# Routing the last tile in halves, the first rows group by group, and an earlier ask for the second expert's weights

## The reference

```python
x = x + mix @ w_out[l]                                    # 512 x 1024
xn = rmsnorm(x, ffn_norm_w)
logits = xn @ w_router + b_router                         # 512 x 32
top_val, top_idx = lax.top_k(logits, 4); gates = softmax(top_val)
# every (token, expert) pair, sorted by expert:
hid = x_blk @ w_gate_up[e] + b_gate_up[e]                 # 1024 -> 2048
gate, up = min(hid[:, :1024], 7), clip(hid[:, 1024:], -7, 7)
y = ((up + 1) * gate * sigmoid(1.702 * gate)) @ w_down[e] + b_down[e]
x = x + segment_sum(y * gate_of_pair, token)
out = rmsnorm(x, final_norm_w)
```

## Time and profile before

| | |
|---|---|
| time, median of 3 runs | 1390.28 us (1388.48 to 1390.84) |
| profiled execution | 1390.32 us, span 1388.6 us |
| TensorE (PE) busy | 1232.1 us (89%) |
| VectorE (DVE) busy | 683.6 us (49%) |
| ScalarE (ACT) busy | 220.4 us (16%) |
| GpSimd (POOL) busy | 327.2 us (24%) |
| chain that ended last | PE 53%, DMA 36%, DVE 7% |
| HBM read, written | 445.02 MB, 14.81 MB |
| mean granted TensorE clock | 0.978 |

### The profile page before, as it was taken

How to read it: one execution, slowest core, us unless ns; L and a number is a source line. 1 busy time by engine, 2 the same in 40 slices (tenths; PEclk the granted TensorE clock), 3 DMA queues, 4 the chain that set the end, 5 groups by cost and what they waited for, 6 DMA issues and landing times.

```text
span 1388.6 us, 32055 instructions
## 1 busy us (share of the span) xinstructions
PE 1232.1 (89%) x12818; PEld 540.9 (39%) x12819; DVE 683.6 (49%) x1365; ACT 220.4 (16%) x435; POOL 327.2 (24%) x435
## 2 busy tenths in 40 slices
PE   6999999999599999799899899788987887879992
PEld 3444555564234443244433334233432332334331
DVE  2898884444543453436433334445443334354428
ACT  3125545313100010000010000000100000001103
POOL 6002111001222233222323222222222222222221
PEclk9999999999799999999999999999999999999996
DMA  9212000511689999999999999999999999999996
GB/s 307 87 61 92 1 31 1 201 73 46 252 339 401 410 418 424 425 427 426 425 426 424 424 427 427 424 427 425 425 424 426 425 426 427 426 425 425 379 409 248
DMA packets 58142, 455.33 MB, mean 328 GB/s; under 512 B 12060, under 2 KB 22356, under 8 KB 32982
## 3 DMA queue, kind: packets, MB, share of 16 engines
q1 hardware_dynamic: 44660, 434.13, 75.5%
q0 software_dynamic: 11664, 18.95, 3.8%
q10 hardware_dynamic: 1778, 1.69, 0.4%
HBM read 445.02 MB, written 14.81 MB: 331 GB/s over the span
## 4 chain that ended last, share of the span: by engine, by line
PE 53%; DMA 36%; DVE 7%; issue 2%; ACT 2%; POOL 1%; SPq 0%; POOLq 0%; DVEq 0%; ACTq 0%
DMA ring<-in_w_gate_up_dram 26%; PE bank L2166 23%; PE bank L2219 11%; DMA dslots<-in_w_down_dram 8%; PE bank L1826 6%; PE bank L2017 4%; DVE dslots L1145 2%; PE bank L1821 2%; DVE hbuf L1720 1%; PE bank L1894 1%; PE bank L1901 1%; DMA rows<-in_x_dram 1%; DMA wq<-xn_rows,idx_in 1%; PE bank L2152 1%; PE bank L1982 1%
## 5 line engine op out<-in xcount | busy, mean ns | idle before, releaser
L2166 PE MATMUL bank<-ring,wq 128*32 128x512 f32 x4992 | 561.2, 598 | 69.6 <-DMA ring<-in_w_gate_up_dram 66.9
L2166 PEld LDWEIGHTS bank<-ring,wq 128*32 128x32 f32 x4992 | 167.8, 110 | 422.7 <-issue 419.7
L2219 PE MATMUL bank<-dslots,intra 128*32 128x256 f32 x5056 | 281.7, 380 | 24.8 <-DMA dslots<-in_w_down_dram 24.6
L2219 PEld LDWEIGHTS bank<-dslots,intra 128*32 128x32 f32 x5056 | 165.0, 110 | 151.4 <-issue 53.9
L1533 DVE TENSOR_REDUCE small<-bank 128x4 f32<-128x8 f32 x33 | 5.5, 166 | 415.7 <-PE bank L2130 415.7
L1012 ACT ACTIVATE zrows<-intra 128x1024 f32<-128x1024 f32 x31 | 32.8, 1058 | 796.8 <-DVE intra L1626 796.8
L1826 PE MATMUL bank<-hbuf,ring 128*128 128x512 f32 x320 | 148.5, 604 | 0.1
L619 POOL COPY idx_in<-idx 128x4 int32 (+1 forms) x32 | 11.9, 371 | 557.8 <-DVE wq L1511 535.4
L1598 DVE STREAM_TRANSPOSE wq<-bank 128x512 f32<-128x512 f32 x124 | 77.8, 685 | 71.0 <-PE bank L2166 71.0
L624 POOL DMA_INDIRECT wq<-xn_rows,idx_in x82 | 101.7, 1241 | 44.2 <-POOL idx_in L619 27.8
L629 POOL DMA_INDIRECT y_rows<-rows,idx_out x79 | 81.2, 1027 | 55.8 <-issue 43.6
(11 more groups left out here) (302 smaller groups left out, 900.6 us busy)
## 6 DMA issues: line engine op xcount, KB each, us to landing
ring<-in_w_gate_up_dram SPq DMA_DIRECT2D x127, 2048.0 KB, 24.9
dslots<-in_w_down_dram SPq DMA_DIRECT2D x61, 2048.0 KB, 25.4
ring<-in_w_in_dram SPq DMA_DIRECT2D x12, 1024.0 KB, 12.4
ring<-in_w_out_dram SPq DMA_DIRECT2D x4, 1024.0 KB, 4.9
ring<-in_w_down_dram SPq DMA_DIRECT2D x4, 1024.0 KB, 24.8
dslots<-y_rows SPq DMA_DIRECT2D x2, 2048.0 KB, 20.2
rows<-in_x_dram SPq DMA_DIRECT2D x4, 512.0 KB, 9.8
hbuf<-in_x_dram SPq DMA_DIRECT2D x4, 512.0 KB, 5.5
```

What stands on the lines that cost most here:

```text
L2166: ins = M(bank[g][GROUP * j:GROUP * (j + 1), :], x[:, g, c * GROUP:(c + 1) * GROUP], w[:, :, j * QD:(j + 1) * QD], start=(c == 0), stop=(c ...
L2219: ins = M(b[GROUP * j:GROUP * (j + 1), col:col + QD], actT[:, g, c * GROUP:(c + 1) * GROUP], w[:, cc, j * QD:(j + 1) * QD], start=(c == 0 ...
```

## The change

- **Logits.** `logits_turn` is a matmul with the folded identity `fold_e` that adds the four partial sums at once; `route` has no reduce any more. The mask is made by one compare of 4 x 32 and one max-reduce.
- **Last tile in halves.** TensorE transposes the first half of the last tile as soon as the first half of the residual is there. Both halves of the transposes are copied by VectorE, and ScalarE's copy of them goes; ScalarE squares the tile when both halves of the residual are there.
- **Places tile by tile.** Ranks, places, `pos` and the one-hots of expert 0 are made for each tile behind its mask; the rank now counts within the tile. The index matmuls of visit 0 leave out the gates (3 columns instead of 6) and are summed in one bank as the tiles come; the gates follow in matmuls of their own (`first_gates`) behind c0 = 0 of visit 0. `split` of the last tile moves behind the gathers.
- **First rows group by group.** The first gather has a semaphore of its own (`lead_in`); groups 0 and 1 are transposed one by one, 2 and 3 together, and TensorE starts with group 0.
- **Index matmuls of visit 1** stand behind c0 = 2 of visit 0 instead of c0 = 0; VectorE makes expert 1's one-hots behind the first transposes.
- **Weights.** SP asks for 1/4 directly behind 0/6, without waiting for the writes of `xn`.
- **Last rows.** The last tile's write to `xn_dram` is issued on ScalarE's queue. Several small loads are counted on other semaphores.

```diff
             gate_up(0, 6)
-            for i in range(2):
-                sp.wait_ge(xn_out[i], 16 * T // 2)
             gate_up(1, 4)
-            sp.wait_ge(first_in, 32)
+            sp.wait_ge(lead_in, 16)
+            sp.wait_ge(first_in, 16)
             sp.wait_ge(gathered, 32)
...
             pool.wait_ge(idx_ready, 1)
             pool.sem_inc(rows_known, 1)
-            for i in range(2):
-                pool.wait_ge(xn_out[i], 16 * T // 2)
-            for g in range(2):
-                gather(g, idx, first_in)
+            pool.wait_ge(xn_out[0], 32)
+            pool.wait_ge(xn_out[1], 16)
+            pool.wait_ge(wr_in, 80)
+            gather(0, idx, lead_in)
+            gather(1, idx, first_in)
             for g in range(2, GROUPS):
                 gather(g, idx)
+            split(T - 1)
...
             x2_square(3)
-            xnT_copy(3)
             x2_rstd(3)
             lgT_copy(3)
+            act.wait_ge(xn_ready, T)
+            act.dma_start(xn_dram[(T - 1) * P:T * P, :], xn[:, (T - 1) % 2, :]).then_inc(wr_in, 16)
             top_exp(3)
...
-                own.mark(V.tensor_scalar(hits, iota_e, pr4[:, 0:1], None, ALU.is_equal))
-                for k in range(1, TOP_K):
-                    own.settle()
-                    ins = V.scalar_tensor_tensor(out=hits if k < TOP_K - 1 else Msk[:, t, :], in0=iota_e,
-                                                 scalar=pr4[:, k:k + 1], in1=hits, op0=ALU.is_equal, op1=ALU.add)
...
+                own.mark(V.tensor_tensor(same, iota_e.rearrange("p (o e) -> p o e", o=1).to_broadcast([P, TOP_K, E]),
+                                         pr4.rearrange("p (k o) -> p k o", o=1).to_broadcast([P, TOP_K, E]),
+                                         ALU.is_equal))
+                own.settle()
+                V.tensor_reduce(Msk[:, t, :], same.rearrange("p k e -> p e k"), AX_X, ALU.max).then_inc(gate_ready, 1)
+
+            def ranks(t):
+                now = rank[:, t * E:(t + 1) * E]
+                dve.wait_ge(gate_ready, t + 1)
+                own.mark(V.tensor_tensor_scan(now, ones16[:, 0:E], Msk[:, t, :], 0.0, ALU.mult, ALU.add))
+                own.settle()
+                own.mark(V.tensor_scalar(view(tg, 0, T, E, 6)[:, t, :, 2:3].rearrange("p e o -> p (e o)"), now,
+                                         float(PAST), float(-PAST), ALU.mult, ALU.add))
...
             residual(3)
-            dve.wait_ge(xn_turned, T)
-            V.tensor_copy(xnT[(T - 1) % 2][:, 4:8, :], view(bank[4], 0, 4, P)).then_inc(xnT_half, 1)
+            dve.wait_ge(lgT_done, T - 2)
+            for half in range(2):
+                dve.wait_ge(xn_turned, T + half)
+                V.tensor_copy(xnT[(T - 1) % 2][:, 4 * half:4 * half + 4, :], view(bank[3 + half], 0, 4, P)
+                              ).then_inc(xnT_half, 1)
+            ranks(2)
+            places(2, 1, 2)
+            hot_tile(0, 2)
             normed(3)
             route(3)
+            ranks(3)
+            places(3, 1, 3)
+            hot_tile(0, 3)
             gates_of(3)
...
-            dve.wait_ge(first_in, 32)
-            first_turn(0)
+            dve.wait_ge(lead_in, 16)
+            first_turn(0, 1, row_turned)
+            dve.wait_ge(first_in, 16)
+            first_turn(1, 1, xt_ready)
             dve.wait_ge(gathered, 32)
-            first_turn(1)
+            first_turn(2, 2, xt_ready)
+            dve.wait_ge(pos_done, 5)
+            hot(1)
...
                     if first and c0 == 0:
-                        pe.wait_ge(idx_ready, 1)
+                        first_gates()
+                    if first and c0 == 2:
                         idx_mm(1, 2 * T + 1)
```

More of the change, by code:

```diff
@@ L195, in block_kernel @@
         rowf = take(GROUPS)
-        fold = take(2 * H)
+        fold_e = take(E)
+        fold = fold_e[:, 0:2 * H]
         leftf, cnt = take(E), take(E)
@@ L1471, in _ @@
             gates_of(0)
+            ranks(0)
             normed(2)
@@ L1533, in numbers @@
                 mk(V.tensor_reduce(rowf, ps[:, :, 0:2], AX_X, ALU.add))
-                mk(V.tensor_reduce(gates[:, bass.ds(stage * GROUPS, GROUPS)], ps[:, :, 2:5], AX_X, ALU.add))
+                mk(V.tensor_reduce(gates[:, bass.ds(stage * GROUPS, GROUPS)], ps[:, :, 3:6], AX_X, ALU.add))
                 dve.wait_ge(s, c)
@@ L1568, in _ @@
             dve.sem_inc(route_ready, 1)
-            hot(1)
-            dve.wait_ge(hot_ready, 2 * T + 1)
-            lower(1)
             def add_bias(t):
@@ L2054, in logits_turn, with places @@
                     pe.wait_ge(mx_ready, t)
-                TR(bank[6][:, 0:P], lgT, ident).then_inc(lg_done, 1)
+                M(bank[6][:, 0:E], lgT, fold_e, start=True, stop=True).then_inc(lg_done, 1)
+            def places(t):
+                pe.wait_ge(gate_ready, t + 1)
+                for u in range(t + 1):
+                    ins = M(bank[1][:, t * E:(t + 1) * E], tri16 if u == t else ones16, Msk[:, u, :], start=(u == 0),
+                            stop=(u == t))
+                return ins
             su(0)
```

179 lines of the change are left out of this document (100 added, 79 removed).

## The result

The changed kernel takes **1394.93 us** (median of 6 runs, 1394.10 to 1395.38) against 1390.32 us for the kernel before in the same comparison: ratio 1.0035, 95% interval 1.0024 to 1.0045. It is slower by 4.6 us, more than the 0.2% that counts; the forecast was 1391.9 us with a range to 1394.8, and "slower" had a chance of 0.21. The profiled execution took 1394.6 us for a span of 1392.8.

The account below looks back on a forecast made before the run. The prediction took the DMA weight stream to bound the kernel, its end set by the queue's last dry spell. Write and gathers 0.6 plus clock 1.0 gave +1.6 us, forecast 1391.9 us, range 1387.2 to 1394.8.

Parts of the forecast that it names:

- The frame: Whole kernel: the end is the weights' queue's last dry spell, ended by ask 2/0, plus a fixed amount of bytes.
- The routing: Last tile's routing: last normalized tile stays at 357.8 us, row numbers ready at about 361.7, 2.9 us earlier.
- The write: Last rows' write to DRAM: shares the engines with the 1/4 transfer, lands at 365.5; first gather 0.6 us later.
- Visit 0: Start of visit 0's matmuls: at 369.1 us, 2.0 us earlier, from group-by-group rows and a 2.2 us gather.
- The gathers of visit 1: Rows for visit 1: land at 394.6, 1.5 us behind the dry queue; visit 1 starts 0.6 us later, at 397.7.
- rival 2: Visit 1's gathers land a fixed 8.95 us after the ask, at 398.0; time 1394.2 to 1396 us; chance 0.12.
- the quick write (1): Last rows' write takes 3.8 us, first gather 2.9 us earlier; time 1387.4, or 1388.4 if the clock falls; chance 0.17.
- the start of visit 0 decides (3): Visit 1's gathers land before TensorE finishes visit 0, so visit 1 follows at 394.5; time 1387.7 us; chance 0.10.
- Rival 4: Clock falls in full and the write lands at its upper bound; 1393 to 1394 us; a fifth of the main case.
- The clock: TensorE's clock after its 3.9 us stop before visit 1: 2.1 us lost if it falls, else nothing; 1.0 taken.
- The step that failed: Visit 1's start to the end: 2/0 asked for 5.6 us after it, any shift passing one for one to the end.
- The place of the index products: Visit 1's index matmuls two weight rows later in visit 0: last gather starts at 389.0 instead of 385.07.

Follow-up runs that it names:

- e1: Changed kernel plus seven dummy product calls on TensorE in its stop before visit 1; 1397.09 us, ratio 1.0047 to the kernel before.
- a1: Changed kernel, but the ask for weight rows 4 and 5 of visit 1 waits for the last rows' write; 1391.27 us, ratio 1.0008 to before.
- c1: Changed kernel with visit 1's index products and the gate products made before visit 0; 1389.64 us, ratio 0.9996 to the kernel before.
- j1: Kernel before with only visit 1's index products moved behind the second pair of weight rows of visit 0; 1391.96 us, ratio 1.0018.
- d1: Changed kernel with the edits of both a1 and c1; 1388.17 us, ratio 0.9981 to the kernel before.
- g1: d1 plus four dummy products on TensorE while it waits for visit 0's first rows; 1386.66 us, ratio 0.9977 to the kernel before.
- h1: Changed kernel with the sync queue's loop turned, its first ask (2/0) written out ahead of it; 1394.16 us, ratio 1.0036 to before.
- p2: Kernel before with 48 already satisfied waits on TensorE's queue ahead of visit 0; 1390.73 us, ratio 1.0003.
- k2: Changed kernel with e2's three dummy products and h1's turned sync loop; 1393.65 us, ratio 1.0025 to the kernel before.
- e2: Changed kernel plus three dummy product calls on TensorE in its stop before visit 1; 1394.07 us, ratio 1.0028 to the kernel before.
- b1: Kernel before with only the early ask for weight rows 4 and 5 of visit 1, write still on GpSimd's queue; 1391.93 us, ratio 1.0016.
- f1: d1's edits, but weight rows 4 and 5 of visit 1 asked for after the first gathered group lands; 1392.33 us, ratio 1.0015 to before.

## Why the prediction was wrong, step by step

**The frame was right.** The end is the last dry spell of the weights' queue plus a fixed amount of bytes, and that spell ends with 2/0. The rates of the stretches show it, and the fourteen kernels follow it within 1.5 us but for e1. The rate of 410 to 427 GB/s does not hold to the end as the prediction said: the last three slices of the page of before read 379, 409 and 248 GB/s.

**The routing** came out as forecast or a little better: the last normalized tile ends at 357.25 (forecast 357.8, lower bound 357.3), the row numbers are ready at 361.0 (361.7), 6 us before the gather that needs them.

**The write** was forecast to land at 365.5 on the sum of the bytes; it landed at 366.1. (2.9 less 1.2 us is 1.7 us of start and receipt and not 1.5, so the sum's own terms give 365.7.) The Trainium skill (DMA: Bandwidth & Descriptors, Queues, rings and completion order) has each engine take turns between its queues by packets, and the prediction drew from it that the write might be out about a microsecond before the stream. The trace agrees with the turns and not with what was drawn from them. Two DMA views of the changed kernel, 360.5 to 365 us and 365 to 366.1 us (queue: packets, MB, share of the 16 engines; q1 is the stream, q10 the write and the down bias behind it):

```profile
q1 hardware_dynamic: 82, 1.33, 76.6%
q10 hardware_dynamic: 85, 0.35, 18.8%
...
q10 hardware_dynamic: 107, 0.31, 69.4%
q1 hardware_dynamic: 15, 0.00, 0.8%
```

One packet of 4 KB of the write's queue goes for each of 16 KB of the stream. But the first packet of the write shows at 360.7, 3.4 us after the ask (1.7 us in a1, 1.1 before), when 2.87 of the stream's 4.19 MB are through. So the stream is through at 365.0, and the other half of the write's queue goes alone, until 366. The sum of the bytes was the right rule, and the turns gain the write nothing. Why the first packet comes so late isn't shown. In the single microseconds no byte moves any more after 366, and the write lands at 366.09:

```profile
365.00:366.00 1.00, 0.00 (x0) 0.00 (x0) 0.00 (x0) 1.00 (x1) 0.00 (x0) 0.50 0.77 307
366.00:367.00 1.00, 0.00 (x0) 0.00 (x0) 0.00 (x0) 0.10 (x1) 0.00 (x0) 0.50 0.00 0
```

**Visit 0** started at 370.66 instead of 369.1. Its terms were each too small: the write by 0.6, the step to the first gather by 0.15, the transpose by 0.1, and a gather alone in its queue, 2.9 us and not 2.2. The 2.2 came from the last of a train of four; the row that bore on it was the 2.86 of the earlier trace rows.

**The gathers of visit 1** were held to land 1.5 us behind the end of the queue's bytes, whatever the time of the ask. That rule is wrong. In c1, where the last is asked for at 379.49, they land at 388.8 with the stream at 459 GB/s and dry only after 392. What the runs show is a time after the ask that depends on the stream: about 9 us where it runs all or nearly all the while (8.95 before, 9.3 in c1), 5.3 us where it runs dry under way (the changed kernel, and j1 with nothing else changed). So 5.2 us of later ask became 1.6 us of later landing (395.58 for 394.02), 1.0 more than the 394.6 of the forecast, and visit 1 moved by 1.49 us and not 0.6. My rival 2 had the fixed 8.95 us after the ask (398), which holds only for the early asks. The ask itself came at 390.28 and not 389.0, because visit 0 started 1.56 us behind its forecast.

Of the other rivals, the quick write (1) did not come: 8.8 us and not 3.8. That the start of visit 0 decides (3) did not either, but it is what c1, d1 and g1 make true: there visit 1 starts right behind visit 0. Rival 4, the clock falling in full with the write near its upper bound, comes nearest to what was measured, but its 1393 to 1394 has no term for the late ask either.

**The clock** was put at 1.0 us between 0 and 2.1. It fell, and cost 1.69 us. What it does isn't the same from run to run: h1 stood 2.42 us and kept the full clock, a1 stood 2.47 us and lost it. The Trainium skill (TensorE: Matmul & The Clock Gate, Part 1: The HAM clock gate (the "warmup" mystery)) says that the point at which the clock moves varies with the phase of a window that runs free of the kernel; these two stops, of nearly one length with opposite outcomes, are in line with it. It may also be why the runs of a1 and j1 spread over some 5 us; with one trace of each, that isn't shown.

**The step that failed** is the last one of the sum, "it comes 5.6 us after TensorE begins visit 1" and "any shift of it goes one for one to the end". The 5.6 us were taken as a constant. They became 8.98: 1.69 for the clock and 1.67 that the forecast has no term for, the ask coming 2.07 us behind its freed slot instead of 0.40. The forecast's +1.6 against the +4.85 of the ask is then 0.9 too little for the start of visit 1, 0.7 too little for the clock, and 1.7 for the late ask. What makes the ask late stays open. It is 0.40 in the kernel before and between 0.65 and 2.34 in every other kernel; all of these kernels, p2 too, have other code than before, and h1 and k2 do not agree on a cure. e2 shows the other side: taking 1.69 us of low clock away moved the ask by 2.15 us, but the stream's lag at 1300 us by 1.1 and the time by only 0.9.

**The place of the index products** was in the sum only as the loss of an earlier start, a move of visit 1 by 0.6 us. j1 puts its price at 0.18% if it is made alone. What it costs beside the early ask isn't measured by itself: c1 is 5.3 us below the changed kernel, but moves the products further forward than they stood before. The early ask costs 1.9 us alone (b1) and 3.7 us in the company of the other (a1). The two shares overlap, since both feed the same stop of TensorE.

## What to carry to other kernels

When a stream is fed through a ring, find the ask after which its queue stays full, and account for every microsecond from the start of the work that frees its slot to that ask: start, clock, and the delay of the asking queue itself. A short write or gather on which a chain depends can land as late as the bulk transfer beside it or later. Holding the bulk back behind the write helped here (a1 against the changed kernel), behind a gather as well it did not (f1). Place the small products that feed the next gathers ahead of the long work, not in it. Bytes moved by a fixed moment, read from a table of windows, tell where a change was won or lost, and here gave the end of the same execution to about 1.5 us.

## What was not expected of the hardware

TensorE stands 0.2 to 0.9 us at the head of a visit in some builds, with no wait to show for it; 48 satisfied waits ahead of the loop brought such gaps into the kernel before (0, then 0.87 us) and cut the changed kernel's from 0.66 to 0.25 us. p2's time is that of before within 0.12%, so while the weights' queue is full this costs nothing that can be measured.

A write of 512 KB took 8.8 and 9.0 us beside a 2 MB transfer, on either queue, where it took 3.8 beside a 128 KB load. It got a packet for each of the stream's, 85 to 82, but a quarter of the bytes, and only from 3.4 us after its ask. A gather of one group took 2.9 us in an empty queue, 7.6 us beside such a transfer, and about 9 us in the middle of the weight stream.

Dummy products kept TensorE's clock up across a wait: visit 1 came 1.9 us earlier (g1 over d1), and 144 matmuls took 15.66 us and not 17.35 (e2). In the time of the kernel the medians give 1.5 and 0.9 us, neither told apart from nothing.
